# Half-size weight slots, later splits, tile sums on VectorE and a third bank pair in the four FFNs of a two-layer transformer

## The chip, the core and the metric

The kernel runs on one NeuronCore of a Trainium2 chip. The metric is device time in microseconds of one execution; the figure for a kernel is the median of its runs.

## What is computed

A two-layer backbone works on 768 tokens of width 1024: 512 latent tokens and 256 context tokens. Each layer is FFN, mixer, FFN, all three with a modulated RMS norm in front and a gated residual behind:

```python
def swiglu(x, w_up, w_down):
    gate, up = jnp.split(x @ w_up, 2, -1)
    return (jax.nn.silu(gate) * up) @ w_down
```

`w_up` is 1024 x 5632 and `w_down` is 2816 x 1024, in float32. The modulation terms are `silu(s) @ w + b` with a vector `s` (nine terms of 1024 for each layer), and they have to be computed as well. The mixers (attention, gated DeltaNet) are not touched by the change. The last FFN works on the 512 latent tokens alone.

## The kernel before, in words

**Numbers.** Every float32 operand is split in a high and a low part that TensorE takes as fp32r, and every product step is three matmuls: high x high, high x low, low x high. So each weight tile costs one pass for the high (`wh`, on ScalarE, line 1245) and one for the low (`wl`, on GpSimd, line 1128, for gate, up and down tiles, or on VectorE, line 1784, for block products).

**One FFN.** The 22 chunks of 128 hidden columns are done in six parts of 4, 2, 4, 4, 4 and 4 chunks (`PARTS`). The chunks of part 0 are plain products: `gate` then `up`, eight steps each. The other 18 chunks use seven block products P1 to P7 in place of eight (one level of a Strassen-like scheme over the halves of K and of the tokens). Their order is P6, P7, P1 of the next chunk, P5, P2 of the next, P4, P3. After each part come its eight `down` products, one for each 128 columns of the output, with as many steps as the part has chunks.

**What a block chunk needs.** Four quarters of weights, 512 x 128 each: A11 and A12 of gate, A21 and A22 of up. VectorE makes four sums of them in place (`quarter_sum`, lines 1753 to 1768), ScalarE seven highs, VectorE seven lows (`pair_lows`, 1784). ScalarE copies four products out of PSUM (`hold_product`, 1266) and applies silu in two halves (1272, 1280). VectorE adds the results (`gate_first` 1717, `up_halves` 1725 and 1728) and gates them (1736, `glu_done`). ScalarE then makes the high of the gated tile (`glu_high`, 1287) and VectorE its low (`gated_low`, 1704 and 1707), which the downs multiply.

**Tile sums.** The block products also want sums and differences of the input tiles. In part 0 VectorE makes tiles from `h` (`t_make`, 1808 and 1810), GpSimd adds them (`t_sums`, four instructions for each of four pairs, 1138 to 1144; `t3_sum`, one for each of four pairs, 1150), ScalarE splits the highs, VectorE the lows.

**Order.** Each engine walks the same list of items (one per product) and does at item i what its tables say. On ScalarE and VectorE an item starts with the weight splits that are due, four items ahead of their use, and the item's own work follows. Residual updates `h` (2238) are made by VectorE after each down; a `down` may start only when its bank pair has been emptied. The downs alternate over two bank pairs, and at the start of a part the first two (`first_downs`) do all steps but their last together, so that the last gated tile may come late.

**Loads.** SyncE issues the loads in order. There are four raw slots of 512 KB; a block chunk takes two of them (gate and up), and both come free with the low of P3, the last one of the chunk. Downs take a whole slot each too. Modulation weights (`ada`, 512 KB each) are loaded between them into their own three buffers, and VectorE multiplies each by two vectors (two instructions on 128 x 1024, line 1984) at items chosen by `ada_plan`.

## Time and profile before

| | |
|---|---|
| median of 3 runs | 3135.46 us (3134.25 to 3136.09) |
| profiled execution | 3134.36 us |
| its span | 3132.6 us |
| busy: TensorE / VectorE / ScalarE / GpSimd | 2881.3 / 2239.7 / 1261.9 / 731.9 us |
| FFN of layer 0, first | about 58 to 632 us |
| mixer of layer 0 | about 632 to 1297 us |
| FFN of layer 0, second | 1297 to 1863 us |
| FFN of layer 1, first | 1864 to 2420 us |
| mixer of layer 1 | about 2430 to 2694 us |
| FFN of layer 1, second (latent tokens) | 2694 to 3119 us |

The profile is one execution. Where two times are given with a colon they are microseconds from the start of its span. "PE" is TensorE's matmul, "PEld" its weight load, DVE is VectorE, ACT ScalarE, POOL GpSimd and SP SyncE. A row of an instruction gives its start, its length, the engine, the line of the kernel, the operation, the tiles, and in brackets how long the engine idled before it and what released it. "PEclk" is TensorE's granted clock as a share of full speed.

### The profile page before, as it was taken

The numbers are of one execution on the slowest core, as the hardware profiler recorded it, in microseconds if no ns is written. First come the engines' busy times: TensorE is split into PE (matmuls) and PEld (weight loads), VectorE is DVE, ScalarE is ACT, GpSimd is POOL, SyncE is SP. The second block draws the span as 40 slices with busy tenths as digits, with TensorE's granted clock in tenths as the row PEclk, the third lists the DMA queues.
The fourth block names the chain that finished last, engine by engine and source line by source line (L and its number), as shares of the span: only waits on it lengthen the run. The fifth ranks groups of instructions, "written<-read, shape, count | busy, mean of one in ns | idle before, by whom it ended". The sixth has DMA issues, their size and how long they took to land. (4 is left out here: it accounts for less than half of the span.)

```text
span 3132.6 us, 48113 instructions
## 1 busy us (share of the span) xinstructions
PE 2881.3 (92%) x18175; PEld 2668.8 (85%) x18175; DVE 2239.7 (71%) x3733; ACT 1261.9 (40%) x2458; POOL 731.9 (23%) x588
## 2 busy tenths in 40 slices
PE   8699999999999988989999999999999989988888
PEld 8588889899888877978999889899998877967787
DVE  7987777885646665698777788877778366676666
ACT  4234333453454455333343343343334256433334
POOL 1501011133332214350110125010112334521111
PEclk9899999999999999999999999999999999999999
DMA  6324244323320022222322321232332300222222
GB/s 242 95 96 134 80 123 129 102 77 120 123 70 15 8 88 78 90 86 75 128 91 91 115 88 61 101 128 75 124 113 83 104 8 22 76 79 82 81 81 81
DMA packets 140227, 285.46 MB, mean 91 GB/s; under 512 B 41774, under 2 KB 63198, under 8 KB 139870
## 3 DMA queue, kind: packets, MB, share of 16 engines
q1 hardware_dynamic: 137262, 275.98, 26.9%
q10 hardware_dynamic: 2736, 6.40, 0.5%
q8 instruction: 147, 2.41, 0.3%
q14 instruction: 82, 0.67, 0.1%
HBM read 270.73 MB, written 15.10 MB: 91 GB/s over the span
## 5 line engine op out<-in xcount | busy, mean ns | idle before, releaser
L1128 POOL TENSOR_TENSOR wl<-raw,wh 128x512 fp32r<-128x512 f32 (+3 forms) x278 | 477.6, 1718 | 1987.2 <-ACT wh L1245 1982.4
L1245 ACT ACTIVATE wh<-raw 128x512 fp32r<-128x512 f32 (+2 forms) x713 | 469.8, 668 | 563.9 <-DMA raw<-in_w 308.1
L2277 PE MATMUL psum<-uh,wh 128*128 128x256 f32 (+5 forms) x1552 | 404.3, 342 | 66.2 <-DVE h L2238 26.5
L2277 PE MATMUL psum<-ul,wh 128*128 128x256 f32 (+5 forms) x1552 | 397.9, 338 | 0.0
L2277 PE MATMUL psum<-uh,wl 128*128 128x256 f32 (+5 forms) x1552 | 397.4, 338 | 0.0
L1984 DVE SCALAR_TENSOR_TENSOR ada_product<-ada_w,cb 128x1024 f32<-128x1024 f32 x256 | 359.5, 1404 | 33.7 <-DMA ada_w<-in_ada_w 28.8
L2277 PE MATMUL psum<-ah,wh 128*128 128x512 f32 (+4 forms) x1040 | 308.2, 359 | 72.3 <-DVE h L2238 21.9
L1784 DVE TENSOR_TENSOR wl<-raw,wh 128x512 fp32r<-128x512 f32 x432 | 293.6, 687 | 104.6 <-ACT wh L1245 102.3
L2238 DVE SCALAR_TENSOR_TENSOR h<-psum,mod,h 128x512 f32<-128x512 f32 x360 | 214.4, 632 | 196.7 <-PE psum L2277 195.7
L2277 PEld LDWEIGHTS psum<-uh,wh 128*128 128x128 f32 (+1 forms) x1552 | 258.3, 191 | 99.4 <-DVE h L2238 35.0
L2293 PE MATMUL psum<-uh,wh 128*128 128x386 f32 (+3 forms) x864 | 281.7, 326 | 37.6 <-ACT held L1266 24.0
L2277 PE MATMUL psum<-al,wh 128*128 128x512 f32 (+4 forms) x1040 | 300.4, 351 | 0.0
L2277 PE MATMUL psum<-ah,wl 128*128 128x512 f32 (+4 forms) x1040 | 300.3, 352 | 0.0
L2293 PE MATMUL psum<-ah,wh 128*128 128x384 f32 (+3 forms) x864 | 286.1, 331 | 8.0 <-ACT held L1266 6.8
L2293 PE MATMUL psum<-al,wh 128*128 128x384 f32 (+3 forms) x864 | 284.8, 330 | 0.0
L2293 PE MATMUL psum<-ah,wl 128*128 128x384 f32 (+3 forms) x864 | 284.3, 329 | 0.0
L2293 PE MATMUL psum<-uh,wl 128*128 128x386 f32 (+3 forms) x864 | 279.3, 323 | 0.0
L2293 PE MATMUL psum<-ul,wh 128*128 128x386 f32 (+3 forms) x864 | 278.7, 323 | 0.0
L2277 PEld LDWEIGHTS psum<-ul,wh 128*128 128x128 f32 (+1 forms) x1552 | 258.8, 191 | 20.4
L2277 PEld LDWEIGHTS psum<-uh,wl 128*128 128x128 f32 (+1 forms) x1552 | 258.6, 191 | 20.4
L2277 PEld LDWEIGHTS psum<-ah,wh 128*128 128x128 f32 x1040 | 183.0, 194 | 107.2 <-DVE h L2238 30.3
L2293 PEld LDWEIGHTS psum<-uh,wh 128*128 128x128 f32 x864 | 165.6, 192 | 43.0 <-ACT held L1266 26.1
(324 smaller groups left out, 5223.2 us busy)
## 6 DMA issues: line engine op xcount, KB each, us to landing
raw<-in_w SPq DMA_DIRECT2D x232, 512.0 KB, 3.9
ada_w<-in_ada_w SPq DMA_DIRECT2D x128, 512.0 KB, 3.8
raw<-in_w SPq DMA_DIRECT2D x160, 256.0 KB, 2.7
spill<-cacc ACTq DMA_DIRECT2D x16, 384.0 KB, 2.4
scale_w<-in_scale_w SPq DMA_DIRECT2D x8, 512.0 KB, 14.7
raw<-in_w SPq DMA_DIRECT2D x32, 128.0 KB, 2.1
ada_w<-bias_final SPq DMA_DIRECT2D x16, 256.0 KB, 3.0
ada_start<-in_ada_w SPq DMA_DIRECT2D x7, 512.0 KB, 15.8
```

The costliest lines, as they stand in the source:

```text
L1128: nc.gpsimd.tensor_tensor(weight_tile(x, wl), raw[raw_place[slot_of[x]][0]][:, 0:n], weight_tile(x, wh).bitcast(f32), ALU.subtract).then_i ...
L1245: nc.scalar.activation(weight_tile(x, wh), src, ACT.Copy).then_inc(hi_split, 1)
L1784: nc.vector.tensor_tensor(weight_tile(x, wl), pair_weight(x), weight_tile(x, wh).bitcast(f32), ALU.subtract).then_inc(pair_lo, 1)
L1984: nc.vector.scalar_tensor_tensor(out=product[:, :], in0=w[:, :], scalar=1.0, in1=cb[:, v, :], op0=ALU.mult, op1=ALU.mult, accum_out=mod[:, ...
L2238: ins = nc.vector.scalar_tensor_tensor(out=h[:, k, lo:hi], in0=banks_of(x)[:, lo:hi], scalar=mod[:, x[1], gate_term(x), k, v:v + 1], in1=h ...
L2277: ins = nc.tensor.matmul(pair[0:w, lo:hi], wt[:, k * w:(k + 1) * w], xt[:, k, cols], start=first, stop=last)
L2293: ins = nc.tensor.matmul(bank, wt[:, tile], xt, start=first, stop=last, skip_group_check=not fresh)
```

## The change

1. **Half slots.** The four raw slots become eight halves. A block chunk takes four halves, one per quarter, each freed by the low of the last product that reads it (A11 by P7, A12 by P3, A21 by P5, A22 by P4). A down takes a half; gate and up take two neighbouring halves.
2. **ScalarE's order.** `glu_high` and `silu_first` of an item stand ahead of the weight splits due at it, and no longer behind.
3. **VectorE's order.** `pair_lows`, with the quarter sums in it, moves from the start of an item to its end, behind gating, up halves, gated low and residual.
4. **Tile sums.** All 20 per FFN move from GpSimd to VectorE, directly behind `t_make`, and the tables of part 0 shift by an item.
5. **Downs over three bank pairs**: (4,5), (6,7) and (bank of the part's last chunk's parity, 3). At the start of a part the first down does all steps but its last, then the second opens (three steps in part 0, up to two elsewhere), and the third opens with one step where a part has two chunks. The first down no longer waits for the second one's banks.
6. **Modulation products** are placed in halves (one instruction each), and stand at P7 and P5 and in downs of parts 1 to 4 only. In the first FFN of each layer the downs of a part carry 12 or 13 halves and the last part none, where they carried 10, 8, 10, 10 and 6; the chunks of a part carry 4 to 7, where they carried 4 to 10.
7. A few semaphores are merged.

```diff
+PAIR_QUARTER = {"P1": "A11", "P7": "A11", "P2": "A12", "P3": "A12", "P5": "A21", "P4": "A22"}
...
         for c, chunk in enumerate(chunks):
-            plan.setdefault(chosen[len(chosen) * c // len(chunks)], []).append(chunk)
+            for v in range(2):
+                plan.setdefault(chosen[len(chosen) * (2 * c + v) // (2 * len(chunks))], []).append((chunk, v))
 
     def shares(x):
         if x[0] == "down":
-            return 2
-        return {"gate": 1, "up": 1, "P7": 1, "P1": 1, "P2": 1}.get(x[0], 0)
+            return 2 if x[3] + 1 < len(PARTS) else 0
+        return {"P7": 1, "P5": 1}.get(x[0], 0)
 
...
-        return [i for i in at[:-2] for _ in range(shares(items[i]))]
+        return [i for i in at for _ in range(shares(items[i]))]
...
+QUARTERS = {"A11": ("gate", 0, "P7"), "A12": ("gate", 1, "P3"), "A21": ("up", 0, "P5"), "A22": ("up", 1, "P4")}
...
-            out += [(("gate",) + x[1:], KD, P), (("up",) + x[1:], KD, P)]
+            out += [((a,) + x[1:], HALF_K, P) for a in QUARTERS]
...
+        if k * w > QUARTER:
+            first = 2 * min(range(RAW_SLOTS), key=lambda r: max(freed[2 * r:2 * r + 2]))
+            mine = [first, first + 1]
+        else:
+            mine = [freed.index(min(freed))]
+        counts[mine[0]] += 1
+        places.append((mine[0], counts[mine[0]], sorted({tenants[b] for b in mine if tenants[b] is not None})))
+        for b in mine:
+            tenants[b] = n
+            freed[b] = number[(QUARTERS[x[0]][2],) + x[1:]] if x[0] in QUARTERS else number[x]
...
+        def down_banks(x):
+
+            p, last = down_at(x) % 3, sum(PARTS[:x[3] + 1]) - 1
+            return (4 + 2 * p, 5 + 2 * p) if p < 2 else (last % 2, 3)
...
+        def raw_tile(n):
+            _, k, w = slots[n]
+            b = raw_place[n][0]
+            return raw[b // 2][:, QUARTER * (b % 2):QUARTER * (b % 2) + k * w]
 
...
-                    T_MAKE.update({at("up", 0): 0, at("gate", 1): 1, at("gate", 2): 2, at("up", 2): 3})
-                    T_HIGHS.update({at("up", 1): 0, at("gate", 2): 1, at("gate", 3): 2, at("up", 3): 3})
-                    T_LOWS.update({at("gate", 2): 0, at("up", 2): 1, at("up", 3): 2, downs[0]: 3})
+                    T_MAKE.update({at("up", 0): 0, at("gate", 1): 1, at("gate", 2): 2, at("gate", 3): 3})
+                    T_HIGHS.update({at("gate", 1): 0, at("up", 1): 1, at("up", 2): 2, at("up", 3): 3})
+                    T_LOWS.update({at("up", 1): 0, at("up", 2): 1, at("up", 3): 2, downs[0]: 3})
...
-                    _, k, w = slots[n]
-                    r, _, tenant = raw_place[n]
-                    if tenant is not None:
-                        sp.wait_ge(*raw_freed(tenant))
+                    b, _, freed_by = raw_place[n]
+                    for m in freed_by:
+                        sp.wait_ge(*raw_freed(m))
                     src = a["w"][slot_at[n]:slot_at[n + 1]].rearrange("(p c) -> p c", p=P)
-                    sp.dma_start(raw[r][:, 0:k * w], src).then_inc(raw_loaded[r], 16)
+                    sp.dma_start(raw_tile(n), src).then_inc(raw_loaded[b], 16)
                 weights_asked[0] = max(weights_asked[0], last + 1)
 
...
-                split_up_to(i)
                 if i and items[i - 1][0] == "P3":
                     glu_high(items[i - 1])
                 if x in silu_first_at:
                     silu_first(silu_first_at[x])
+                split_up_to(i)
...
                     silu_second(x)
-                if x in T_HIGHS:
+                if x[0] == "down" and x in T_HIGHS:
...
+            def t_sums(x, j):
+
+                n = T_STEPS * ffn_no(x) + 5 * j + 1
+                (ua, ub), (va, vb) = ([t[:, cols] for cols in halves(x)] for t in uv[j % 2])
+                near = ua[:, 0:width_of(halves(x)[1])]
+                dve.wait_ge(t_added, n)
+                nc.vector.tensor_tensor(vb, vb, ub, ALU.subtract).then_inc(t_added, 1)
+                dve.wait_ge(t_added, n + 1)
+                nc.vector.tensor_tensor(ub, ub, near, ALU.subtract).then_inc(t_added, 1)
+                dve.wait_ge(t_added, n + 2)
+                nc.vector.tensor_tensor(near, near, vb, ALU.add).then_inc(t_added, 1)
+                dve.wait_ge(t_added, n + 3)
+                nc.vector.tensor_tensor(va, va, ua, ALU.subtract).then_inc(t_added, 1)
+
+            def t3_sum(x, j):
+
+                ub, vb = (t[:, halves(x)[1]] for t in uv[j % 2])
+                dve.wait_ge(t_added, T_STEPS * ffn_no(x) + 5 * HALF_K + 2 * j + 1)
+                nc.vector.tensor_tensor(ub, vb, ub, ALU.subtract).then_inc(t_added, 1)
 
...
-                pair_lows(i)
                 before_x = items[i - 1] if i else x
                 if before_x[0] == "P3":
                     gated_second(before_x)
@@ -2060,15 +2083,14 @@
                     up_halves(x)
                 if x in low_at:
                     gated_low(low_at[x])
-                if x in T_LOWS:
-                    t_lows(x, T_LOWS[x])
-                if x in T_MAKE:
-                    t_make(x, T_MAKE[x])
-                if x[0] == "down" and x[3] == 0 and down_at(x) < HALF_K + 2:
-                    if down_at(x) >= 2:
+                if x[0] == "down" and x[3] == 0:
+                    if x in T_LOWS:
+                        t_lows(x, T_LOWS[x])
+                    if 2 <= down_at(x) < HALF_K + 2:
                         u_lows(x, down_at(x) - 2)
                     if down_at(x) < HALF_K:
                         t_make(x, HALF_K + down_at(x))
+                        t3_sum(x, down_at(x))
                 if x[0] == "norm":
                     m = norm_no[x]
...
                     if x not in put_off:
                         finish_product(x)
+                    if x in T_LOWS:
+                        t_lows(x, T_LOWS[x])
+                    if x in T_MAKE:
+                        t_make(x, T_MAKE[x])
+                        t_sums(x, T_MAKE[x])
...
+                pair_lows(i)
+                for c, v in plan.get(i, []):
+                    ada_half(c, v)
+                    if v and c[2] == KD - 1:
                         ada_term(*c[:2])
 
...
+            def open_down(y):
+
+                for z in before[y]:
+                    for signal in released(z):
+                        pe.wait_ge(*signal)
+                pe.wait_ge(lo_split, low_no[y] + 1)
+
+            def first_downs(x, others):
 
                 first = glu_no[next(y for y in items if y[0] in ("up", "P3") and y[1:4] == x[1:4])[1:]]
                 last = PARTS[x[3]] - 1
-                for y in before[second]:
-                    for signal in released(y):
-                        pe.wait_ge(*signal)
-                for y in (x, second):
-                    pe.wait_ge(lo_split, low_no[y] + 1)
-                    for k in range(last):
-                        if y == x:
-                            pe.wait_ge(a_lo, first + k + 1)
+                pe.wait_ge(lo_split, low_no[x] + 1)
+                for k in range(last):
+                    pe.wait_ge(a_lo, first + k + 1)
+                    dense_step(x, k, *a_of(x))
+                for y in others:
+                    open_down(y)
+                    for k in range(begun(y)):
                         dense_step(y, k, *a_of(y))
                 pe.wait_ge(a_lo, first + last + 1)
 
+            def begun(y):
+
+                n = PARTS[y[3]]
+                if down_at(y) == 0:
+                    return n - 1
+                if down_at(y) == 1:
+                    return n - 1 if y[3] == 0 else min(n - 1, 2)
+                return int(n == 2 and down_at(y) == 2)
+
             def start_scale(k):
...
-                    if x[0] == "down" and down_at(x) < 2:
+                    if x[0] == "down" and begun(x):
                         if down_at(x) == 0:
-                            first_downs(x, items[i + 1])
-                        dense_step(x, PARTS[x[3]] - 1, *a_of(x)).then_inc(product_done, 1)
+                            first_downs(x, [y for y in items[i + 1:i + 3] if begun(y)])
+                        for k in range(begun(x), PARTS[x[3]]):
+                            ins = dense_step(x, k, *a_of(x))
+                        ins.then_inc(product_done, 1)
```

The products on TensorE, their steps and their order are unchanged. What the change moves is seen on the other engines at three places.

VectorE in the last FFN, one stretch of a steady block chunk, before (`raw` tiles are quarters, 1725 to 1736 are `up_halves` and its gating, 1764 is the sum for P5, 1768 that for P3):

```order
L1764 TENSOR_TENSOR raw2<-raw2 128x512 [waits summed]
L1784 TENSOR_TENSOR wl2<-raw0,wh2 128x512 [waits hi_split]
L1725 TENSOR_TENSOR sq<-held,sq 128x256 [waits held_copied]
L1728 TENSOR_TENSOR sq<-held,psum 128x258 [waits a_lo,product_done]
L1736 SCALAR_TENSOR_TENSOR sq<-sq 128x256 [waits silu_done,quarter_added]
L1784 TENSOR_TENSOR wl2<-raw2,wh2 128x512 [waits hi_split]
L1784 TENSOR_TENSOR wl0<-raw0,wh0 128x512 [waits hi_split]
L1736 SCALAR_TENSOR_TENSOR sq<-sq 128x256 [waits silu_done]
L1717 TENSOR_TENSOR sq<-held,psum 128x258 [waits glu_done,held_copied,product_done]
```

and after (the same functions have moved four lines down; 1768 is the sum for P5, 1772 that for P3):

```order
L1788 TENSOR_TENSOR wl2<-raw3,wh2 128x512 [waits hi_split]
L1729 TENSOR_TENSOR sq<-held,sq 128x256 [waits held_copied]
L1732 TENSOR_TENSOR sq<-held,psum 128x258 [waits a_lo,product_done]
L1740 SCALAR_TENSOR_TENSOR sq<-sq 128x256 [waits silu_done,quarter_added]
L1768 TENSOR_TENSOR raw0<-raw0 128x512 [waits summed]
L1788 TENSOR_TENSOR wl2<-raw1,wh2 128x512 [waits hi_split]
L1788 TENSOR_TENSOR wl0<-raw0,wh0 128x512 [waits hi_split]
L1740 SCALAR_TENSOR_TENSOR sq<-sq 128x256 [waits silu_done]
L1721 TENSOR_TENSOR sq<-held,psum 128x258 [waits glu_done,held_copied,product_done]
L1788 TENSOR_TENSOR wl0<-raw2,wh0 128x512 [waits hi_split]
```

The sum for P5 has moved from ahead of `up_halves` to behind the gated half.

ScalarE in the last FFN, from the second silu half of the last chunk of a part (1280) on, before:

```order
L1280 ACTIVATE sq<-psum,sq 128x256 [waits glu_done,product_done]
L1245 ACTIVATE wh1<-raw0 128x512 [waits product_done,raw_loaded0]
L1287 ACTIVATE ah<-sq 128x512 [waits glu_done]
L1245 ACTIVATE wh1<-raw3 128x512 [waits product_done,raw_loaded3]
L1245 ACTIVATE wh2<-raw0 128x512 [waits product_done,raw_loaded0]
L1245 ACTIVATE wh2<-raw3 128x512 [waits product_done,raw_loaded3]
L1245 ACTIVATE wh0<-held 128x512 [waits product_done,summed]
L1245 ACTIVATE wh0<-raw1 128x512 [waits product_done,summed]
```

and after:

```order
L1282 ACTIVATE sq<-psum,sq 128x256 [waits glu_done,product_done]
L1289 ACTIVATE ah<-sq 128x512 [waits glu_done]
L1247 ACTIVATE wh1<-raw3 128x512 [waits product_done,raw_loaded6]
L1247 ACTIVATE wh1<-raw0 128x512 [waits product_done,raw_loaded0]
L1247 ACTIVATE wh2<-raw0 128x512 [waits product_done,raw_loaded1]
L1247 ACTIVATE wh2<-raw3 128x512 [waits product_done,raw_loaded7]
L1247 ACTIVATE wh0<-held 128x512 [waits product_done,summed]
L1247 ACTIVATE wh0<-raw1 128x512 [waits product_done,summed]
```

The high of the gated tile (1287, now 1289) stands directly behind the silu half, ahead of the split of a down's weights.

VectorE in the first FFN, four of part 1's eight downs, before (2238 is a residual update in two segments, 1984 a modulation half):

```order
L2238 SCALAR_TENSOR_TENSOR h<-psum,mod,h 128x512 [waits h_updated,mod_ready,product_done]
L2238 SCALAR_TENSOR_TENSOR h<-psum,mod,h 128x256
L1984 SCALAR_TENSOR_TENSOR ada_product,mod<-ada_w1,cb 128x1024 [waits ada_summed,ada_loaded1]
L1984 SCALAR_TENSOR_TENSOR ada_product,mod<-ada_w1,cb 128x1024 [waits ada_summed]
L2238 SCALAR_TENSOR_TENSOR h<-psum,mod,h 128x512 [waits h_updated,mod_ready,product_done]
L2238 SCALAR_TENSOR_TENSOR h<-psum,mod,h 128x256
L2238 SCALAR_TENSOR_TENSOR h<-psum,mod,h 128x512 [waits h_updated,mod_ready,product_done]
L2238 SCALAR_TENSOR_TENSOR h<-psum,mod,h 128x256
L1984 SCALAR_TENSOR_TENSOR ada_product,mod<-ada_w2,cb 128x1024 [waits ada_summed,ada_loaded2]
L1984 SCALAR_TENSOR_TENSOR ada_product,mod<-ada_w2,cb 128x1024 [waits ada_summed]
L2238 SCALAR_TENSOR_TENSOR h<-psum,mod,h 128x512 [waits h_updated,mod_ready,product_done]
L2238 SCALAR_TENSOR_TENSOR h<-psum,mod,h 128x256
```

and after (2266 and 2005 are the same lines):

```order
L2266 SCALAR_TENSOR_TENSOR h<-psum,mod,h 128x512 [waits h_updated,mod_ready,product_done]
L2266 SCALAR_TENSOR_TENSOR h<-psum,mod,h 128x256
L2005 SCALAR_TENSOR_TENSOR ada_product,mod<-ada_w0,cb 128x1024 [waits ada_summed,ada_loaded0]
L2266 SCALAR_TENSOR_TENSOR h<-psum,mod,h 128x512 [waits h_updated,mod_ready,product_done]
L2266 SCALAR_TENSOR_TENSOR h<-psum,mod,h 128x256
L2005 SCALAR_TENSOR_TENSOR ada_product,mod<-ada_w0,cb 128x1024 [waits ada_summed,ada_loaded0]
L2005 SCALAR_TENSOR_TENSOR ada_product,mod<-ada_w1,cb 128x1024 [waits ada_summed,ada_loaded1]
L2266 SCALAR_TENSOR_TENSOR h<-psum,mod,h 128x512 [waits h_updated,mod_ready,product_done]
L2266 SCALAR_TENSOR_TENSOR h<-psum,mod,h 128x256
L2005 SCALAR_TENSOR_TENSOR ada_product,mod<-ada_w1,cb 128x1024 [waits ada_summed,ada_loaded1]
L2266 SCALAR_TENSOR_TENSOR h<-psum,mod,h 128x512 [waits h_updated,mod_ready,product_done]
L2266 SCALAR_TENSOR_TENSOR h<-psum,mod,h 128x256
```

Between two residual updates stand one or two modulation halves now, where there were none or two.

## Rows read from the trace of the kernel before

**Rows 1.** Waits of PE in the whole span: total us, times, longest us

```profile
PE psum L2277 <- DVE h L2238: 48.4, 39, 4.4
PE psum L2293 <- ACT held L1266: 30.8, 12, 7.1
PE psum L2277 <- DVE ul L1707: 24.9, 9, 8.0
...
PE psum L2277 <- DVE al L1704: 18.6, 5, 5.2
...
PE psum L2293 <- DVE sq L1728: 14.7, 12, 2.0
```

**Rows 2.** Windows (length, busy PE PEld DVE ACT POOL, PEclk, DMA, GB/s), parts 1 to 5

```profile
169.91:632.02 462.11, 430.75 (x2378) 404.44 (x2377) 361.77 (x587) 172.96 (x328) 59.65 (x41) 0.98 0.36 111
1420.44:1863.36 442.92, 426.06 (x2378) 402.17 (x2376) 342.43 (x553) 172.88 (x328) 59.68 (x41) 0.99 0.30 100
1973.58:2420.43 446.85, 427.09 (x2378) 402.02 (x2376) 361.36 (x587) 171.92 (x328) 55.99 (x41) 0.99 0.31 105
2774.55:3119.31 344.76, 303.62 (x1946) 275.87 (x1945) 217.46 (x349) 143.51 (x296) 49.63 (x42) 0.94 0.23 77
```

**Rows 3.** The same view, part 0 of each FFN with its downs

```profile
58.19:169.91 111.72, 81.74 (x433) 75.14 (x433) 102.73 (x144) 30.40 (x49) 48.70 (x33) 0.89 0.32 101
1297.00:1420.44 123.44, 108.37 (x582) 101.33 (x581) 114.43 (x150) 38.16 (x58) 58.96 (x35) 0.94 0.26 82
1863.63:1973.58 109.95, 103.85 (x580) 97.98 (x581) 86.58 (x119) 38.18 (x58) 50.05 (x35) 1.00 0.21 68
2694.38:2774.55 80.17, 72.57 (x484) 65.24 (x482) 66.63 (x87) 31.97 (x54) 44.18 (x35) 0.98 0.24 73
```

**Rows 4.** The same view: undisturbed block chunk (full width, last FFN), four downs

```profile
453.98:468.74 14.76, 14.76 (x86) 14.76 (x85) 13.00 (x23) 7.72 (x15) 0.00 (x0) 1.00 0.46 126
2829.07:2839.09 10.02, 10.02 (x87) 10.02 (x86) 9.09 (x17) 5.31 (x12) 0.00 (x0) 1.00 0.14 35
...
519.19:536.09 16.90, 16.90 (x99) 14.79 (x97) 12.63 (x25) 2.53 (x4) 0.00 (x0) 1.00 0.45 129
```

**Rows 5.** The page's costliest groups: ScalarE's weight splits and their wait

```profile
L1245 ACT ACTIVATE wh<-raw 128x512 fp32r<-128x512 f32 (+2 forms) x713 | 469.8, 668 | 563.9 <-DMA raw<-in_w 308.1
```

**Rows 6.** Timeline: first chunk after a part's downs, and its first matmul

```profile
398.59 0.63 ACT L1245 ACTIVATE wh<-raw 128x512 fp32r<-128x512 f32 x1 [8.79 <-DMA raw<-in_w]
...
399.65 0.69 PE L2293 MATMUL psum<-uh,wh 128*128 128x384 f32 x1 [7.06 <-ACT held L1266]
```

**Rows 7.** Timeline of ScalarE, last FFN: splits for a block chunk

```profile
2840.26 1.15 ACT L1245 ACTIVATE wh<-raw 128x512 fp32r<-128x512 f32 x2 [2.47 <-DMA raw<-in_w]
```

**Rows 8.** The page's DMA issues: count, KB each, median us to landing

```profile
raw<-in_w SPq DMA_DIRECT2D x232, 512.0 KB, 3.9
...
raw<-in_w SPq DMA_DIRECT2D x160, 256.0 KB, 2.7
```

**Rows 9.** Timeline and window of part 1's eight downs, first FFN

```profile
208.48 0.62 PE L2277 MATMUL psum<-ah,wh 128*128 128x512 f32 x2 [2.58 <-DVE al L1707]
...
203.66:227.50 23.84, 18.15 (x98) 14.71 (x98) 19.40 (x31) 4.82 (x10) 4.67 (x6) 1.00 0.59 195
...
228.76 1.13 DVE L2238 SCALAR_TENSOR_TENSOR h<-psum,mod,h 128x512 f32<-128x512 f32 x2
```

**Rows 10.** Timeline of part 0: residual wait, modulation half beside a GpSimd split

```profile
1389.73 0.80 PE L2277 MATMUL psum<-uh,wh 128*128 128x512 f32 x1 [4.43 <-DVE h L2238]
...
80.14 3.29 DVE L1984 SCALAR_TENSOR_TENSOR ada_product<-ada_w,cb 128x1024 f32<-128x1024 f32 x1
...
78.98 3.37 POOL L1128 TENSOR_TENSOR wl<-raw,wh 128x1024 fp32r<-128x1024 f32 x1
```

**Rows 11.** VectorE's groups: modulation products; a 384-column addition

```profile
L1984 DVE SCALAR_TENSOR_TENSOR ada_product<-ada_w,cb 128x1024 f32<-128x1024 f32 x256 | 359.5, 1404 | 33.7 <-DMA ada_w<-in_ada_w 28.8
...
L1725 DVE TENSOR_TENSOR sq<-held,sq 128x384 f32<-128x384 f32 x54 | 39.5, 731 | 22.3 <-ACT held L1266 22.3
```

164 lines of the change are left out of this document (72 added, 92 removed).

## The prediction, made before the changed kernel had run

> **What bounds the kernel now.** I read the waits of PE first [rows 1], then windows over the four FFNs [rows 2, 3], then single stretches. PE is busy for 2881 of 3132.6 us, so the change, which leaves PE's instructions alone, can take only idle time of PE and time lost to a lower clock. The mixers are not touched. In the FFNs an undisturbed block chunk takes 14.76 us at full width and 10.02 us in the last FFN, with PE busy throughout, and four downs of four chunks 16.90 us, so 4.23 us each [rows 4]; a down of two chunks takes half, and in the last FFN (512 of 768 columns) two thirds, 2.82 us.
>
> Parts 1 to 5 would then need 18 x 14.76 + 32 x 4.23 + 8 x 2.11 = 418 us at full width and 18 x 10.02 + 32 x 2.82 + 8 x 1.41 = 282 us in the last FFN. They took 462.1, 442.9, 446.8 and 344.8 [rows 2]: an excess of 44, 25, 29 and 63 us, 161 in all. Length less PE's busy time gives idle PE of 31.4, 16.9, 19.8 and 41.1 us, 109 in all. The other 52 is time at half clock: PEclk is 0.94 in the last FFN, and 6% of 344.8 is 21 us, as is 63 less 41. Part 0: a plain product has eight steps, so 8.45 us (5.64 in the last FFN). Five of them are left in the first window, eight in the others; with eight downs and 1 us for the norm this makes 76, 102.5, 102.5 and 69 us against 111.7, 123.4, 110.0 and 80.2 [rows 3]: an excess of 36, 21, 7 and 11 us, 75 in all, of which 59 is idle PE. So the prize is 236 us, and the question is how much of each excess goes.
>
> **Half slots (1), and ScalarE's order (2).** ScalarE waits 308 us for raw weights [rows 5]. At a part's end this reaches PE: the split for the new chunk came 8.79 us late, the copy of a product stands behind it on ScalarE, and PE waited 7.06 us for that copy [rows 6]. Within the last FFN the same happens in each chunk at a smaller size: ScalarE idles 2.47 us for a load [rows 7], VectorE's low follows, `up_halves` stands behind that low, and PE waits (the row of L1728, 14.7 us in 12 waits). The cause is in the code: both tiles of a chunk are freed by the low of P3, its last one. Now A11 is freed by P7's low and A21 by P5's, half a chunk (some 7 us) sooner, and downs take half a slot, so a chunk has twice the places. Loads of 256 KB land 2.7 us after their issue, those of 512 KB in 3.9 [rows 8], far less than 7. I take both stalls at nothing in steady chunks, and `glu_high` ahead of the splits removes the part of the gated-low wait that came from queueing (al L1704, ul L1707).
>
> The Trainium skill ("DMA: Bandwidth & Descriptors", section "Anatomy of one DMA — SWDGE (gpsimd) path") prices a DMA at some 2 us fixed beside its bytes, and the two times above agree with a fixed part. If four quarters came one after the other at 2.7 us they would need 10.8 us a chunk against 7.8 for two halves; in the last FFN, at 11.0 us a chunk, that would just fit, so the sum stays.
>
> **VectorE's order (3).** In a full-width chunk VectorE is busy 13.00 us of 14.76 [rows 4]. Its work per chunk stays, and its waits for ScalarE's highs come to about 1.1 to 1.4 us, so its cycle is 14.1 to 14.4, still under PE's. In the last FFN it is busy 9.09 of 10.02. There the sum for P5 now stands behind the gated half. ScalarE's next split waits for that sum, its silu half stands behind, and the copy of P6's successor behind that. I count four waits of VectorE for a ScalarE split on the way, about 0.35, 0.95, 0.1 and 0.4 us (a split takes 0.63 [rows 6], a hop between engines 0.1 to 0.2, an estimate), so the cycle is 9.09 + 1.8 = 10.9, with queueing 11.06, against PE's 10.02. So a **new wait** of 1.04 us a chunk appears before P5. In a part of four the first chunk has slack, the second loses 0.5, the last two 1.06 each: 2.6 us a part, 11 us with the short part.
>
> **Downs (5).** The first downs must wait for the last chunk's gated low. The chain behind P3 is 4.8 us (hop 0.2, silu 0.56, gating 1.35, high 0.85, low 1.66 with hops; estimates from the waits of rows 1 and 9). Cover by steps that can go ahead, 1.06 us each at full width: three of the first down and two of the second, 5.3 us, with n = 4: no wait. With n = 2 it is three steps, 3.2 us: 1.6 us in each full-width FFN (before: 2.58 us [rows 9]). In the last FFN a step takes 0.70 us, so 3.5 and 2.1 us of cover: 5.4 us over five parts, GpSimd's splits beside VectorE's included. Part 1's downs take only 2.11 us each and VectorE has for each a residual update (1.13 + a shorter one in the rows, 1.06 alone [rows 9]), about 1.5 modulation halves now and weight lows. That is 26 us of VectorE against 19 to 21 of PE, three bank pairs or not: 6, 4 and 6 us stay (23.84 us were used for the window, 18.15 of them busy).
>
> **Sum for parts 1 to 5.** Full width: 16 (part 1's downs) + 5 (gated low) + 6 (2 us per FFN for the rest, a guess from how even the middle chunks are) + 10 of half clock, since the clock fell behind long stalls that go = 37 of 98 us; gain 61. Last FFN: 11 + 5.4 + 6 of half clock = 22 of 63; gain 41.
>
> **Tile sums (4) and modulation (6).** VectorE makes 20 more additions in each part 0. The nearest row is 0.73 us for 384 columns [rows 11], some of it beside GpSimd; I take 0.56 each, 11 us per FFN (ends 8 and 15). Against this, GpSimd no longer adds beside VectorE: a modulation half took 3.29 us beside a GpSimd split of 3.37 [rows 10] and 1.40 in the mean [rows 11]. The splits stay; of the contention with the sums I expect 5 to 8 us per FFN back. The Trainium skill ("SBUF — State Buffer", section "Who interferes with whom") has VectorE with two SBUF inputs and GpSimd exclude one another, and the 3.29 agrees. Net VectorE gains 3 to 4 us of work per part 0. VectorE is busy 102.7 of 111.7 in the first [rows 3], so it is the limit there, and PE's waits for residual updates (up to 4.43 us [rows 10]) are its shadow. The third pair lets a down start when the update three before it is done, not two: one down's time, 4.2 us, of slack once per part, and the first down no longer waits for the second's banks. I take 5 + 5 + 3 + 4 = 17 us of 75 (ends: -10, if the sums land on the path, and 30). Modulation halves keep their number (256 instructions); moving them out of the last part's downs costs nothing there.
>
> **Sum.** 61 + 41 + 17 = 119. From 3134.36 this gives 3015.4; the median of the runs stands 1.1 us above it: **3016 us**.
>
> **Rivals.**
> - *No new wait*: the last FFN stays at PE's pace (gain 11 more), part 1's downs are covered (16 more), part 0 gives 30 (13 more), the clock 10 more. 3016 - 50 = 2966. For: VectorE has 0.9 us free per chunk; against: the order of instructions on both engines.
> - *Loads do not come earlier*: SyncE issues in order, and a load whose slot is not free, or a modulation load behind a late buffer, holds all behind it. Then ScalarE's 8.79 us stalls [rows 6] stay for the most part, only the gated-low waits and the banks gain: about 60 us, 3075. For: twice the waits in the queue, and the modulation buffers are released by VectorE later than today. Against: the queue asks in the order of use, and most halves are freed 7 us sooner.
> - *Slower*: VectorE's cycle passes PE's at full width too. It decides above 14.76 us a chunk, and cancels the whole gain when 54 chunks lose 2.2 us each (119 us), so from about 17.0. At 17.5 it is 54 x 2.74 = 148, so 3016 + 148 = 3164. For: 13.00 us busy plus one modulation half of 1.4 in some chunks, each wait for a split added; against: I find only 1.4 us of waits.
> - *No change*: what goes in part ends returns inside the chunks; 3135.
>
> **Chances.** Forecast 0.67 (own range 3000 to 3045), no new wait 0.11, loads late 0.16, slower 0.04, no change 0.02. The range leaves out the last two and the tips of the rivals: 2980 to 3070. A measurement of this kernel tells 0.2% (6 us) from no change: faster 0.94, same 0.02, slower 0.04.
>
> **What would show it.** ScalarE's wait for raw loads falls from 308 us to under 120. The waits of PE for the copy before P3 at part starts and the row of L1728 go; in the last FFN a wait for the copy before P5 appears and chunks there take about 11.0 us, against 14.76 elsewhere. Waits for gated lows fall under 15 us in all. Waits for `h` stay above 20 us, in parts 0 and 1. PEclk of the last FFN's later parts rises from 0.94 to 0.98. The forecast is wrong if full-width chunks take over 15 us, if ScalarE still waits several us at part starts, or if part 0 grows longer.

## The result and the profile after

The changed kernel takes **3019.58 us** (median of four runs, 3018.73 to 3020.68), the kernel before 3135.78 on the same chip: a ratio of 0.963, 95% interval 0.9613 to 0.9647. The forecast was 3016.

Waits of PE in the changed kernel (us in total, times, longest), to be read against [rows 1]; the function of line 2277 is at 2307 now, that of 2293 at 2322:

```profile
PE psum L2307 <- DVE h L2266: 27.2, 16, 6.9
PE psum L2307 <- DVE sq L1694: 15.4, 2, 7.9
...
PE psum L2307 <- DVE ul L1711: 10.7, 1, 10.7
PE psum L2322 <- DVE wl L1788: 9.3, 9, 2.1
PE psum L2322 <- ACT held L1268: 8.6, 8, 3.0
...
PE psum L2307 <- DVE al L1708: 5.6, 5, 1.8
```

Every wait of [rows 1] is smaller: residual updates 48.4 to 27.2 us, the copy 30.8 to 8.6, the two rows of gated lows together 43.5 to 16.3, and the row of `up_halves` (14.7 us) is gone. New among the large ones is the row of L1788, a wait for the low of a block product's weights, 9.3 us. The 10.7 us are one wait, in part 0 of the second FFN, where it was 8.0 before. The same for ScalarE, against [rows 5]:

```profile
ACT wh L1247 <- DVE raw L1768: 295.3, 71, 9.5
ACT wh L1247 <- DMA raw<-in_w: 144.5, 39, 11.3
```

The 308 us for loads have become 144.5, and ScalarE now waits 295 us for the sum for P5 (115.2 before, at line 1764). Most of that hurts nobody; where it does is told below.

Windows of the changed kernel, columns as in [rows 2], from the first block product of an FFN to the norm behind it (the last one to the end of its downs):

```profile
171.71:616.96 445.25, 432.31 (x2426) 409.73 (x2425) 366.23 (x597) 176.93 (x336) 61.98 (x43) 0.99 0.41 121
1400.08:1830.61 430.53, 427.41 (x2427) 406.97 (x2426) 347.17 (x564) 177.65 (x337) 60.11 (x43) 1.00 0.34 106
1930.13:2364.38 434.25, 429.01 (x2427) 408.62 (x2425) 367.00 (x598) 174.10 (x334) 59.44 (x41) 1.00 0.35 113
2707.36:3005.64 298.28, 287.15 (x1946) 262.36 (x1945) 220.03 (x351) 144.23 (x299) 52.02 (x42) 1.00 0.31 89
```

Before, the same stretches took 470.66, 451.74, 456.50 and 344.76 us. The first three are 8.5 to 9.7 us longer than the windows of [rows 2], because the product that runs ahead of the next norm is in them. So parts 1 to 5 gained 25.4 + 21.2 + 22.3 = 68.9 us at full width (61 forecast) and 46.5 in the last FFN (41 forecast). Part 0, from the norm to the first block product:

```profile
55.98:171.71 115.73, 86.93 (x437) 78.81 (x437) 105.62 (x163) 30.87 (x50) 25.10 (x14) 0.88 0.28 93
1283.03:1400.08 117.05, 99.19 (x534) 92.09 (x533) 109.84 (x160) 31.34 (x49) 29.11 (x14) 0.94 0.25 81
1830.61:1930.13 99.52, 96.57 (x533) 90.70 (x533) 87.64 (x128) 31.36 (x49) 26.47 (x14) 0.98 0.20 63
2633.45:2707.36 73.91, 67.75 (x437) 60.37 (x435) 67.07 (x99) 25.76 (x46) 27.35 (x15) 0.95 0.26 79
```

Between the same points it took 114.2, 115.0, 101.4 and 74.4 before: 405.0 us in all, and 406.2 now. Part 0 gained nothing, where 17 us were forecast; the first two grew, by 1.6 and 2.1 us.

The table below is what the experiments are read with. Its cells are times between landmarks of PE's timeline (first matmul after a switch between block products and downs), in us: the block products of a part / its downs. An undisturbed part of four chunks is 59.1 / 33.8 at full width and 40.1 / 22.6 in the last FFN; part 1, with two chunks, is 33.8 / 16.9 and 22.9 / 11.3. In part 5 there is no next chunk whose P1 and P2 would come early, so its products are 54.9 and 37.2, and at full width its downs column holds one product of what follows: 42.2.

| kernel, FFN | part 0 | part 1 | part 2 | part 3 | part 4 | part 5 |
|---|---|---|---|---|---|---|
| before, first | 114.2 | 33.8/23.8 | 65.0/36.1 | 75.0/35.5 | 59.1/37.8 | 54.9/49.6 |
| before, second | 115.0 | 33.8/23.4 | 59.1/38.8 | 59.1/37.5 | 60.3/38.6 | 54.9/46.2 |
| before, third | 101.4 | 33.8/23.4 | 60.5/38.2 | 65.2/35.7 | 59.1/36.2 | 54.9/49.6 |
| before, last | 74.4 | 25.7/18.8 | 48.0/29.6 | 48.1/30.0 | 50.0/28.2 | 43.6/22.8 |
| after, first | 115.7 | 33.8/19.8 | 64.5/33.8 | 62.4/34.3 | 65.5/34.1 | 54.9/42.2 |
| after, second | 117.0 | 33.8/18.4 | 62.2/33.7 | 59.1/33.7 | 59.1/33.7 | 54.8/42.1 |
| after, third | 99.5 | 33.8/19.8 | 64.6/33.7 | 59.1/33.7 | 59.1/33.7 | 54.8/42.1 |
| after, last | 73.9 | 23.6/12.6 | 42.1/23.9 | 42.1/23.9 | 42.2/24.7 | 40.0/23.1 |

### The profile page after: what moved, and what is told of

Same layout as the page of the kernel before. It is cut to its first block, busy times and chain, and to the rows that moved or that the text cites. A ratio compares the mean times of both kernels' runs of the same rounds, so it can differ in the third digit from the quotient of the medians.

```text
span 3018.9 us, 48480 instructions
## 1 busy us (share of the span) xinstructions
PE 2851.4 (94%) x18175; PEld 2653.7 (88%) x18175; DVE 2255.8 (75%) x3813; ACT 1255.2 (42%) x2458; POOL 645.8 (21%) x508
## 4 chain that ended last, share of the span: by engine, by line
PE 70%; DVE 16%; issue 5%; ACT 4%; SPq 2%; DMA 1%; POOL 1%; DVEq 0%; ACTq 0%; POOLq 0%
PE psum L2307 33%; PE psum L2322 26%; DVE ada_product L2005 2%; PE psum L2529 2%; DVE stats L1812 1%; SPq L999 1%; PE psum L2612 1%; DVE o_acc L2136 1%; DVE held L1812 1%; PE psum L2635 1%; DVE h L2266 1%; DVE wl L1788 1%; PE psum L2622 1%; PE psum L2514 1%; DVE sq L1694 1%
## 5 line engine op out<-in xcount | busy, mean ns | idle before, releaser
L1247 ACT ACTIVATE wh<-raw 128x512 fp32r<-128x512 f32 (+2 forms) x713 | 462.3, 665 | 556.6 <-DVE raw L1768 295.3
L2307 PE MATMUL psum<-uh,wh 128*128 128x256 f32 (+5 forms) x1552 | 399.8, 339 | 32.4 <-DVE h L2266 11.6
L2005 DVE SCALAR_TENSOR_TENSOR ada_product<-ada_w,cb 128x1024 f32<-128x1024 f32 x256 | 346.2, 1352 | 21.7 <-DMA ada_w<-in_ada_w 14.4
L1788 DVE TENSOR_TENSOR wl<-raw,wh 128x512 fp32r<-128x512 f32 x432 | 300.9, 697 | 51.3 <-ACT wh L1247 45.7
L2307 PEld LDWEIGHTS psum<-uh,wh 128*128 128x128 f32 (+1 forms) x1552 | 257.0, 190 | 59.2 <-DVE h L2266 14.7
L2307 PEld LDWEIGHTS psum<-ah,wl 128*128 128x128 f32 x1040 | 180.8, 192 | 19.6
## 6 DMA issues: line engine op xcount, KB each, us to landing
scale_w<-in_scale_w SPq DMA_DIRECT2D x8, 512.0 KB, 14.6
```

The source lines that it names most:

```text
L1247: nc.scalar.activation(weight_tile(x, wh), src, ACT.Copy).then_inc(hi_split, 1)
L1788: nc.vector.tensor_tensor(weight_tile(x, wl), pair_weight(x), weight_tile(x, wh).bitcast(f32), ALU.subtract).then_inc(pair_lo, 1)
L2005: nc.vector.scalar_tensor_tensor(out=product[:, :], in0=w[:, :], scalar=1.0, in1=cb[:, v, :], op0=ALU.mult, op1=ALU.mult, accum_out=mod[:, ...
L2307: ins = nc.tensor.matmul(bank, wt[:, k * w:(k + 1) * w], xt[:, k, cols], start=first, stop=last)
```

## The experiments

Each kernel here ran in four runs or five beside the kernel before. The first six undo one part of the change each, or a piece of one; the merged semaphores were not undone. The single runs are compared by their ratios to the kernel before; an interval is some 5 us to each side.

### Half slots undone: 3082.21 us

```diff
-            out += [((a,) + x[1:], HALF_K, P) for a in QUARTERS]
+            out += [(("gate",) + x[1:], KD, P), (("up",) + x[1:], KD, P)]
...
-        if k * w > QUARTER:
+        if k * w > QUARTER or x[0] == "down":
...
-            return pair_lo, pair_low_no[(QUARTERS[x[0]][2],) + x[1:]] + 1
+            return pair_lo, pair_low_no[("P3",) + x[1:]] + 1
```

> The changed kernel with the half slots undone: gate and up of a block chunk as two loads of 512 KB, both freed by the low of P3, and a down takes a whole slot. All else as changed. Theory (as predicted): ScalarE's wait for raw loads comes back from 144.5 to over 280 us, and with it most of the idle PE of parts 1 to 5, so 3019 + 60 to 80 = 3080 to 3100. Rival: the orders on ScalarE and VectorE carry the gain and early loads are worth little: 3020 to 3035.

Ratio to the kernel before 0.9824 (0.9809 to 0.9839), so 62.6 us slower than the changed kernel. ScalarE's wait:

```profile
ACT wh L1248 <- DMA raw<-in_w: 444.8, 164, 11.4
```

Of the 62.6 us, 31 are lost in the last FFN (four chunks take 49.9, 48.2 and 46.8 us in place of 42.1), 8 to 11 in parts 1 to 5 of each other FFN. The theory holds: early loads are, of the parts undone alone, the one that costs most. ScalarE's wait is then longer than the 308.1 us of the kernel before, so half slots are not the only edit that bears on it.

### Order of ScalarE and VectorE undone: 3016.08 us

```diff
+                split_up_to(i)
                 if i and items[i - 1][0] == "P3":
                     glu_high(items[i - 1])
...
+                pair_lows(i)
                 before_x = items[i - 1] if i else x
...
-                pair_lows(i)
                 for c, v in plan.get(i, []):
```

> The changed kernel with the order of both engines undone: weight splits ahead of the item's own work on ScalarE and on VectorE. Theory: the sum for P5 is early again, so the wait before P5 in the last FFN goes (chunk 10.53 to about 10.1 us, 8 us gained), but gated low and residual stand behind the weight lows, and the waits of part ends come back: 15 to 30 us lost; in all 3030 to 3045. Rival: with loads early the order does not matter: 3012 to 3022.

Ratio 0.9611 (0.9597 to 0.9626): the interval overlaps that of the changed kernel, so the new order is worth nothing that can be told. Its first half was as expected: four chunks of the last FFN take 40.2 us, PE's own pace, in place of 42.1. The second was not: instead of 15 to 30 us only a few are lost. The downs behind these chunks take 28.3, 23.5 and 26.5 us in place of 23.9, 23.9 and 24.7.

### The sum for P5 alone put back ahead of `up_halves`: 3017.98 us

```diff
                 elif x[0] == "P4":
+                    up_sum(x)
                     up_halves(x)
```

(`up_sum` makes the next chunk's sum for P5 if it is due at this item.)

> The changed kernel with only the sum for P5 back ahead of up_halves on VectorE; its lows stay at the end of an item. Theory (the new wait of the prediction): the sum behind the gated half is what makes ScalarE's split, and with it the copy that PE waits for, late in the last FFN; a chunk goes from 10.53 to 10.1 us there, so 6 to 8 us are gained, nothing elsewhere: 3011 to 3014. Rival: VectorE's work is the bound in the last FFN (9.3 us busy and the hand-offs), and the sum's place does not matter: 3017 to 3021.

Ratio 0.9615 (0.9599 to 0.9631), no change that can be told. Yet the mechanism is there. In the changed kernel, last FFN, ScalarE waits for the sum in each chunk (2.02, 2.03 us), and PE, in the later chunks of a part, for ScalarE's copy. One of each:

```profile
2830.89 0.63 ACT L1247 ACTIVATE wh<-raw 128x512 fp32r<-128x512 f32 x1 [2.02 <-DVE raw L1768]
...
2844.96 0.39 PE L2322 MATMUL psum<-ah,wh 128*128 128x256 f32 x1 [0.32 <-ACT held L1268]
```

With the sum early, four chunks take 41.0 us in place of 42.1. Where the gain went is seen at the first downs behind them, PE's row in the changed kernel and in this one, and this one's window of those eight downs:

```profile
2790.52 0.50 PE L2307 MATMUL psum<-ah,wh 128*128 128x512 f32 x1 [1.10 <-DVE al L1708]
```

```profile
2789.94 0.80 PE L2316 MATMUL psum<-ah,wh 128*128 128x512 f32 x1 [2.81 <-DVE al L1708]
```

```profile
2783.26:2810.30 27.04, 24.23 (x100) 19.21 (x99) 11.05 (x16) 6.89 (x12) 7.58 (x6) 0.94 0.32 97
```

The chunks end sooner, the gated low does not, and PE waits 2.81 us in place of 1.10. The granted clock of the window is 0.94 in place of 1.00, and the downs take 27.0 us in place of 23.9: the saving of 1.1 us comes back as a loss of 3.1 at this place, 1.7 of it the wait and 1.4 busy time. In the two other parts of four the downs take 0 and 1.6 us more. The 1.6 can't be laid to the sum: the same downs of part 4, with the order as in the changed kernel, take 25.2 us in one run below and 26.5 in another:

```profile
2913.91 0.50 PE L2306 MATMUL psum<-ah,wh 128*128 128x512 f32 x1 [2.42 <-DVE al L1707]
...
2907.85:2933.09 25.24, 22.82 (x98) 18.01 (x97) 10.83 (x15) 6.98 (x12) 7.39 (x6) 1.00 0.33 102
```

```profile
2896.82 0.50 PE L2308 MATMUL psum<-ah,wh 128*128 128x512 f32 x1 [2.18 <-DVE al L1731]
...
2891.01:2917.53 26.52, 24.34 (x98) 19.12 (x97) 10.84 (x15) 6.98 (x12) 7.36 (x6) 0.94 0.31 96
```

(The first is the run that moves one modulation term, the second the one with three edits.) A wait of 2.42 us left the clock at 1.00 there, and one of 2.18 went with 0.94, so the length of the wait alone does not decide it. In part 2, of the runs with half slots, the three with the sum early have the loss (28.3, 27.0, 27.1 us) and all others 23.9 to 24.6.

### Tile sums back on GpSimd: 3003.52 us

```diff
                     if x in T_MAKE:
                         t_make(x, T_MAKE[x])
-                        t_sums(x, T_MAKE[x])
```

and on GpSimd, with a semaphore of its own for `t_make` and the tables of before:

```diff
                 split_up_to(number[x])
+                if x in T_MAKE:
+                    t_sums(x, T_MAKE[x])
+                if x[0] == "down" and x[3] == 0 and down_at(x) < HALF_K:
+                    t3_sum(x, down_at(x))
```

> The changed kernel with the 20 tile sums per FFN back on GpSimd, with the tables of before. Theory 1 (the prediction's): the sums on VectorE are 11 us per FFN, of which 5 to 8 come back as contention, so this run is 3 to 4 us per part 0 faster, 3005 to 3015. Theory 2: what counts is the chain (a sum behind t_make on the same engine, no hop and no slow GpSimd instruction), and this run is slower, 3025 to 3040. Theory 3: no difference, 3017 to 3022.

Ratio 0.9571 (0.9555 to 0.9587): **16 us faster** than the changed kernel, all of it in part 0. Its windows there:

```profile
57.12:166.94 109.82, 84.24 (x437) 76.23 (x437) 101.03 (x142) 29.93 (x48) 53.32 (x34) 0.91 0.31 98
1277.59:1387.85 110.26, 98.53 (x534) 91.36 (x533) 103.53 (x140) 31.34 (x49) 55.50 (x34) 0.97 0.26 85
1818.39:1917.27 98.88, 96.26 (x534) 90.72 (x533) 78.54 (x109) 32.26 (x51) 43.92 (x34) 0.98 0.20 64
2620.46:2691.54 71.08, 66.14 (x436) 59.40 (x435) 56.86 (x79) 25.66 (x46) 42.21 (x35) 0.98 0.27 82
```

Moving the sums to VectorE adds 4.6, 6.3, 9.1 and 10.2 us to its busy time, 30 in all, and part 0 grows by 5.9, 6.8, 0.6 and 2.8 us. Where VectorE is nearly full (the first two), its added work is about part 0's added time. Three additions and one more of the changed kernel, and GpSimd's split beside the last:

```profile
90.25 0.56 DVE L1823 TENSOR_TENSOR held<-held 128x384 f32<-128x384 f32 x1
90.85 0.56 DVE L1825 TENSOR_TENSOR held<-held 128x384 f32<-128x384 f32 x1
91.44 0.56 DVE L1827 TENSOR_TENSOR held<-held 128x384 f32<-128x384 f32 x1
92.03 2.60 DVE L1829 TENSOR_TENSOR held<-held 128x386 f32<-128x386 f32 x1
```

```profile
91.45 2.76 POOL L1153 TENSOR_TENSOR wl<-raw,wh 128x1024 fp32r<-128x1024 f32 x1 [14.05 <-ACT wh L1247]
```

An addition is 0.56 us alone, and 2.60 beside the split. In the last FFN, with 256 columns, it is 0.43 alone:

```profile
L1823 DVE TENSOR_TENSOR held<-held 128x256 f32<-128x256 f32 x2 | 0.8, 425 | 0.1
```

Theory 1 had the sign. Its 3 to 4 us per part 0 is the mean of what came (16.1 / 4), by four places that differ; for VectorE's work it is too small at each.

The 20 additions of an FFN took 13.2, 16.4, 14.2 and 11.6 us on VectorE, where 20 x 0.56 is 11.2 (20 x 0.43 is 8.5 in the last): one to three in each ran beside a split, at 1.4 to 2.8 us. Less the 4.6, 6.3, 9.1 and 10.2 us, VectorE's other work became 8.6, 10.1, 5.1 and 1.4 us shorter, 25 in all.

### Downs over two bank pairs: 3048.14 us

```diff
-            p, last = down_at(x) % 3, sum(PARTS[:x[3] + 1]) - 1
-            return (4 + 2 * p, 5 + 2 * p) if p < 2 else (last % 2, 3)
+            p = down_at(x) % 2
+            return (4 + 2 * p, 5 + 2 * p)
...
+                for y in others:
+                    for z in before[y]:
+                        for signal in released(z):
+                            pe.wait_ge(*signal)
...
-                if down_at(y) == 1:
-                    return n - 1 if y[3] == 0 else min(n - 1, 2)
-                return int(n == 2 and down_at(y) == 2)
+                return n - 1 if down_at(y) == 1 else 0
```

> The changed kernel with downs over two pairs of banks and the first down waiting for the second's. Theory 1 (the prediction's): part 0 loses the 17 us that the third pair was to give, part 1's downs some more: 3036 to 3050. Theory 2: part 0 is bound by VectorE's total work (105.6 busy of 113.3 us in the first FFN), slack moves nothing there, and only part 1's downs lose 3 to 5 us each: 3028 to 3036 with 0 to 3 us from part 0.

Ratio 0.9713 (0.9698 to 0.9727), 28.6 us slower. Its part 0 takes 119.9, 121.2, 105.3 and 78.9 us: 425.2 in place of 406.2, so **the third pair is worth 19 us in part 0**, and theory 1 holds. The other 9 us or so are lost in parts 1 to 5, by 1 to 3 in each FFN. In part 1 it moves time and takes none away. The stretch from part 1's downs to the end of part 2's block products in the second FFN, in the changed kernel and in this one:

```profile
1433.87:1514.47 80.60, 77.48 (x434) 73.59 (x434) 71.52 (x120) 34.22 (x68) 9.51 (x8) 1.00 0.36 112
```

```profile
1444.18:1524.78 80.60, 77.66 (x433) 73.73 (x433) 71.51 (x120) 34.22 (x68) 9.47 (x8) 1.00 0.35 113
```

With three pairs it is 18.4 + 62.2, with two 21.2 + 59.4.

### Modulation products placed as before: 3046.76 us

```diff
-            return 2 if x[3] + 1 < len(PARTS) else 0
-        return {"P7": 1, "P5": 1}.get(x[0], 0)
+            return 2
+        return {"gate": 1, "up": 1, "P7": 1, "P1": 1, "P2": 1}.get(x[0], 0)
```

(and the two halves of a load together again)

> The changed kernel with the old placing of the modulation products: whole chunks (two instructions), also at P1 and P2, also in the last part and its downs. Theory 1: VectorE is the bound around part 1's downs and the chunks behind them, and a plan that puts 10, 8, 10, 10 and 6 halves there in place of 12 or 13 gives back 2 to 4 us in each of three FFNs, but two in a row (2.8 us) delay residual updates and copies: net 3010 to 3025. Theory 2: halves in place of wholes matter, and this run is slower by more than 10 us: above 3030.

Ratio 0.9709 (0.9694 to 0.9723), 27.2 us slower. It is slower by more than theory 2's 10 us, but not for its reason alone. The stretches from part 1's downs to the end of part 2's products gain 2.2, 0.2 and 2.2 us, at or under the low end of theory 1. The loss is elsewhere: the last part's downs take 50.3, 47.0 and 51.0 us in place of 42.2, 42.1 and 42.1 (21.9 us), and the products of parts 3 and 4 of the first FFN 75.9 + 59.1 in place of 62.4 + 65.5 (7.1 us). The last downs of the first FFN in the changed kernel and in this one:

```profile
574.72:616.96 42.24, 42.24 (x241) 37.99 (x241) 29.36 (x45) 22.63 (x35) 12.40 (x8) 1.00 0.22 71
```

```profile
577.45:627.71 50.26, 44.17 (x241) 39.68 (x241) 39.32 (x61) 22.62 (x35) 15.17 (x8) 0.93 0.23 78
```

There VectorE has residual updates, squares and the next norm's lows beside them, so the halves came on top of a busy stretch: 10 us more of VectorE, and PE idle for 6.1 us and partly at half clock.

### Small table writes spread, on the changed kernel: 3012.81 us

```diff
+                if x[0] in PAIR and x[1:3] == (0, 0) and "dnA" in no and x[5] >= 10 and windows:
...
+                    for wnd in windows[:3]:
+                        window(*wnd)
+                    windows = windows[3:]
...
-                        for wnd in windows[:8]:
-                            window(*wnd)
-                        windows = windows[8:]
```

> The changed kernel with the 192 small table writes of SyncE in the first FFN spread: three at each block product from chunk 10 on, in place of eight at each P1 and P2 (up to 16 in a row, 11 us of SyncE). Theory: the modulation load that stands behind the writes comes late, VectorE waits for it (3.94 and 2.47 us) and the next copy reaches PE late (3.01 and 1.76 us); spread, parts 3 and 4 of the first FFN go from 62.4 and 65.5 us to 59.1 each: 3019 - 8 to 10 = 3009 to 3012. Rival: the load's own buffer wait is the cause and nothing moves: 3017 to 3022.

What it tests is this chain of the changed kernel: SyncE, VectorE, PE.

```profile
448.51 10.15 SPq L999 DMA_DIRECT2D bias_hbm<-toeplitz  x16
458.70 0.59 SPq L1042 DMA_DIRECT2D ada_w<-in_ada_w  x1
...
463.03 1.22 DVE L2005 SCALAR_TENSOR_TENSOR ada_product<-ada_w,cb 128x1024 f32<-128x1024 f32 x1 [3.94 <-DMA ada_w<-in_ada_w]
...
466.69 0.44 PE L2322 MATMUL psum<-uh,wh 128*128 128x384 f32 x1 [3.01 <-ACT held L1268]
```

Ratio 0.9602 (0.9588 to 0.9617), 6.8 us faster. The interval just touches that of the changed kernel; the trace has 6.3 us of it at the place, in parts 1 to 5 of the first FFN. Part 3's block products fall from 62.4 to 59.4 us, part 4's from 65.5 to 62.2; the 59.1 expected for both was reached in one.

### The same edit on the kernel before: 3128.75 us

> The kernel before with one edit: SyncE's 192 small table writes spread, three at each block product. The prediction laid ScalarE's 8.79 us wait at a part's end to slots that come free late. Theory 1 (SyncE's 16 writes in a row, 10.7 to 10.9 us, stand ahead of the modulation load that VectorE waits for): part 3 of the first FFN falls from 75.0 to 60 to 64 us, the whole from 3136 to 3122 to 3127. Theory 2 (slots free late): part 3 moves by under 3 us.

Ratio 0.9966 (0.9953 to 0.9979), 8.9 us faster than the kernel before beside it. Part 3 of the first FFN falls from 75.0 to 64.2 us, part 2 from 65.0 to 61.9. SyncE in the kernel before, ahead of the stall of [rows 6]:

```profile
376.78 10.92 SPq L975 DMA_DIRECT2D bias_hbm<-toeplitz  x16
387.75 0.59 SPq L1018 DMA_DIRECT2D ada_w<-in_ada_w  x1
```

Theory 1 holds for the place, and the whole stands just above its 3122 to 3127. But the stall of [rows 6] is not gone. At the same chunk, with the writes spread:

```profile
387.78 0.63 ACT L1245 ACTIVATE wh<-raw 128x512 fp32r<-128x512 f32 x1 [5.37 <-DMA raw<-in_w]
...
388.84 0.44 PE L2293 MATMUL psum<-uh,wh 128*128 128x384 f32 x1 [3.65 <-ACT held L1266]
```

And SyncE's wait for the slot's last low, ahead of this raw load, in the kernel before (388 to 399 us) and in this run (375 to 390 us):

```profile
SPq L943 <- DVE wl L1784: 7.6, 1, 7.6
```

```profile
SPq L943 <- DVE wl L1784: 3.8, 1, 3.8
```

So the raw load did stand for its slot, in both. In the kernel before VectorE's low, which frees it, was itself late: VectorE had waited 3.91 us (at 391.53) for the modulation load that stood behind the writes. The writes make 3.4 of the 8.79 us, and 3.4 of PE's 7.06; what stays comes with SyncE's wait for the slot. The third FFN, which has no such writes, shows the same stall with 4.90 us on ScalarE and 3.14 on PE.

### One modulation term moved out of part 0 of the second FFN: 3011.32 us

```diff
-    over(later_parts(0, 0), ada_chunks(0, range(3, 8)))
-    over(ahead_of_downs(0, 1), ada_chunks(0, [8]))
+    over(later_parts(0, 0), ada_chunks(0, range(3, 9)))
```

> The changed kernel with one modulation term (16 instructions, 8 loads) moved from part 0 of the second FFN to the later parts of the first. Theory: VectorE's total work bounds part 0 there (108.7 of 116.0 us busy), so part 0 of the second FFN shortens by 10 to 16 us, and the first FFN, with 16 more instructions where some stretches have no room, lengthens by 4 to 8: 3008 to 3015. Rival: part 0 is bound by the chain of residual updates and not by the sum of the work: part 0 moves by less than 4 us and the whole is slower, 3020 to 3028.

Ratio 0.9595 (0.9581 to 0.961), 8.3 us faster. The second FFN's part 0:

```profile
1289.88:1389.43 99.55, 95.04 (x534) 89.43 (x534) 87.67 (x128) 31.36 (x49) 26.45 (x14) 1.00 0.20 63
```

VectorE has 22.2 us less to do there (109.84 to 87.67), and the part is 17.5 us shorter, with PE's clock at 1.00. The first FFN is 6.7 us longer in parts 1 to 5. So part 0 was bound by VectorE's total work, as theorised; it shortened by 4.7 us less than that work did, and PE is now busy for 95.04 of its 99.55 us.

### Three edits together: 2993.25 us

Tile sums on GpSimd, table writes spread, the term moved.

> The changed kernel with three edits at once: tile sums back on GpSimd, table writes spread, one modulation term moved from the second FFN's part 0 to the first FFN. Alone they gave 16, 7 and 8 us. If they add up, except for the 6 us that sums and the moved term both take from part 0 of the second FFN: 3019.6 - 25 = 2994 (2989 to 2999). If VectorE's room in the first FFN is used up twice, 3000 or more.

Ratio 0.9537 (0.9521 to 0.9553): 26.3 us faster than the changed kernel. The single results sum to 31, less some 6 that the sums and the moved term both take from one part 0.

### The same with the old order: 2995.44 us

> The kernel with the three edits and the order of before on ScalarE and VectorE. Undone alone, the new order was worth -3.5 us (the old one faster). Theory: it stays so, 2 to 5 us faster than with the three edits. Rival: with more work in the first FFN's chunks the residual updates and gated lows behind the weight splits come late, 3 us or more slower.

Ratio 0.9544 (0.9529 to 0.9558), no difference that can be told. The last FFN's chunks are at PE's pace again (40.1 us for four), and the downs behind them take 27.1, 23.7 and 26.8 us, against 24.2, 23.8 and 26.5 with the new order: only the first place differs.

### And fewer modulation halves around part 1's end: 2977.23 us

```diff
-            return 2 if x[3] + 1 < len(PARTS) else 0
-        return {"P7": 1, "P5": 1}.get(x[0], 0)
+            return {1: 1}.get(x[3], 2) if x[3] + 1 < len(PARTS) else 0
+        return {"P7": 1, "P5": int(x[3] != 2 or x[4] > 1)}.get(x[0], 0) if x[0] != "P7" or x[3] != 2 or x[4] else 0
```

> The kernel with the three edits, and fewer modulation halves around part 1's end: one share instead of two at part 1's downs, none in the first chunk of part 2, one in the second. Theory: part 1's downs and the chunks behind them are one stretch bound by VectorE's total work (18.4 to 19.8 + 62.2 to 64.6 us against 16.9 + 59.1), so some 8 halves of 1.3 us fewer give 4 to 6 us in each of two or three FFNs, and the middle chunks have the room: 2980 to 2988. Rival: the stretch is bound by the chain of a down, its update and the next: under 3 us in all.

Ratio 0.9486 (0.9471 to 0.95), 16 us faster again and **the fastest kernel of the study**, 42 us below the changed one. In the second FFN the stretch that took 80.60 us:

```profile
1406.47:1482.69 76.22, 76.18 (x433) 73.85 (x433) 65.63 (x107) 34.23 (x68) 10.13 (x8) 1.00 0.35 107
```

VectorE's 71.5 us became 65.6, and PE is busy for 76.18 of 76.22. The edit also takes loads out of SyncE's queue: in the changed kernel ScalarE waited 11.0, 5.3 and 11.3 us there for a raw load, where SyncE had waited 17.1, 19.6 and 18.7 us for modulation buffers, and 2.1 us at most now. No run parts the two. For VectorE's work speaks that it was busy for 14.6 of the first 14.77 us of part 2's products in each of the three FFNs. In the third FFN 19.8 + 64.6 became 17.2 + 59.2. In the first, 23.0 + 66.6 became 17.1 + 60.3, of which 5.2 come back in part 3 (60.6 to 65.8), where the halves went.

## Why the prediction was right, and where it was not

**Right in total, by parts that missed both ways.** 61 + 41 + 17 were forecast; 68.9 + 46.5 - 1.3 came, and each mixer moved by about 1 us. Most of what parts 1 to 5 gave above the forecast is the clock, told below.

**Half slots.** Right: undone alone, they cost 62.6 us, and ScalarE waits 444.8 us for loads. The forecast of under 120 us for that wait missed; 144.5 stayed, and waits of 11.0 and 11.3 us at part 1's end are what the rival of late loads names, a modulation load that waits for its buffer ahead of them. One reading was incomplete: the 8.79 and 7.06 us of [rows 6] were laid to slots that come free late. The slot was late, but in part because SyncE's 16 table writes (10.9 us) held back a modulation load and VectorE with it. The run that spreads the writes on the kernel before takes 10.8 us from that part, and leaves 5.37 and 3.65 us of the two waits; the run with half slots but the old modulation plan keeps 75.9 us there. The step skipped was to look at SyncE's own rows at the time of the stall.

**The new wait in the last FFN.** The mechanism was right, and so, nearly, was the size. The later chunks of a part come 10.81 us apart (ScalarE's wait for the sum ends at 2830.89 and 2841.70), where 11.06 was forecast against 10.02. The products of the five parts stand 0.7 + 2.0 + 2.0 + 2.1 + 2.8 = 9.6 us above PE's pace, 11 forecast; the early sum takes 5.1 of them, the old order 6.5. What the sum did not have is that a faster chunk can give this back at the next gated low, as it did in part 2, so the order as a whole is worth nothing that can be told.

**Part 1's downs and what follows.** Forecast: 16 us of residual and 5 for gated lows. Measured over 16.9 a piece: 2.9 + 1.5 + 2.9 = 7.3 in the downs, and 5.4 + 3.1 + 5.5 = 14.0 in the four chunks behind. That is 21.3, with the place wrong: the third pair lets PE run ahead, and VectorE's backlog is met one stage later. "26 us of VectorE against 19 to 21 of PE, three bank pairs or not" was the right reason, with the number spread over two stages: in the first FFN VectorE is busy 16.28 us within these downs and 14.59 of the 14.77 behind them. The last experiment agrees, by taking VectorE's work away.

**Modulation placing: the term that was missing.** The prediction has it that moving halves out of the last part's downs "costs nothing there", and asks no further. It brought 7.4, 4.1 and 7.5 us there (49.6, 46.2 and 49.6 to 42.2, 42.1 and 42.1), 19 of the 69 us at full width. The windows of [rows 2] hold all eight downs, so the excess was counted in the prize, but it was given to other edits. With the old placing alone put back, 21.9 us return there.

**Tile sums and part 0: the step that failed.** 17 us were forecast, -1.3 came, and of the prediction's own signs of being wrong, that part 0 grows longer, one came true in two FFNs. The third pair gave its 19. The sums took 16. The term that was too small is their price: 0.56 us is right for one alone, but the 20 of an FFN took 13.2, 16.4, 14.2 and 11.6 us and not 11, because GpSimd's splits, the long instructions, stay and some additions fell beside them. The relief on VectorE's other work was 25 us in all, within the 5 to 8 per FFN expected, though unevenly (8.6, 10.1, 5.1, 1.4). So VectorE gained 7.5 us of work per part 0 in place of 3 to 4. And the net was not set against a bound: the prediction names VectorE as the limit of part 0 and still books a gain, but where VectorE is busy for 105.6 of 115.7 us, each added microsecond is about a microsecond of part 0 (5.9 and 6.8 for 4.6 and 6.3). Some 4 us of part 0 (-19 + 16 + 4 = 1) are not laid to any edit: the order undone leaves part 0 within 1 us, and what else costs them stays open. So does the remainder of the whole: the five undone parts add up to 62.6 - 3.5 - 16.1 + 28.6 + 27.2 = 98.8 us of 116; where the other 17 come from, two edits that only pay together or the merged semaphores, was not tried.

**Clock.** The terms for half clock, 10 us at full width and 6 in the last FFN, were too large. The windows of parts 1 to 5 are granted 0.99, 1.00, 1.00 and 1.00, which leaves some 5 us in all, an estimate from length times missing clock. That is 11 of the 13.4 us by which these parts beat the forecast. The last FFN had 0.94 before, and 0.98 was forecast.

## What to carry to other kernels

Before crediting more buffers with a gain, add up the work of the engine behind them over the whole stretch: the third bank pair, worth 19 us in part 0, only moved PE's wait around part 1's downs from one stage to the next (80.60 us both ways), while six us less work for VectorE, with fewer loads beside it, took 4.4 us off the same stretch. Work that can stand anywhere, as the modulation halves here, belongs where that engine has room, and its place was worth more than most edits to the critical code (27 and 16 us). And for a wait on a load, read the queue of the engine that issues it: the load may be late for its slot, for what stands ahead of it, or, as here, for both.

## What the runs showed of the hardware

Sixteen small writes issued by SyncE took 10.15 and 10.92 us of its queue, 0.63 to 0.68 us each, and a load behind them waits for all. An addition on VectorE of 0.56 us took 2.60 beside a GpSimd split of 2.76 us. And a wait of 2.81 us in place of 1.10 ahead of eight downs went with a granted clock of 0.94 in their window and 3.1 us more for them, so that a saving of 1 us upstream became a loss; waits of 2.18 and 2.42 us at another place went with 0.94 and 1.00.
